# Two dense blocks on one core: the moving operand of the feature products read in lines 0, 8, 1, 9, with operands and weight parts at multiples of 1024 bytes

## What is computed

```python
h = rms_norm(x, mix_norm_pre) * (1.0 + sc1) + sh1
a_q, a_f, a_i, a_g, b_q, b_k, b_v, c_a, c_g = split_cols(h @ w_in, IN_SPLITS)
...
gates = sigmoid(h @ w_gate + b_gate)
merged = (gates[0] * (ya @ w_a_out) + gates[1] * (yb @ w_b_out) + gates[2] * (yc @ w_c_out))
x = x + g1 * rms_norm(merged @ w_o, mix_norm_post)
h = rms_norm(x, mlp_norm_pre) * (1.0 + sc2) + sh2
y = square(relu(h @ w_up)) @ w_down            # 2048 -> 8192 -> 2048
```

## Time and profile before

| | |
|---|---|
| Runs | 3234.96, 3237.93, 3238.77 us; median 3237.93 |
| Profiled execution | 3238.04 us, its span 3236.2 us |
| Granted TensorE clock | 0.996 of full speed |
| TensorE (matmul) | busy 3175.0 us, 98% of the span, 23,974 matmuls |
| VectorE | 2371.3 us, 73% |
| ScalarE | 1333.7 us, 41% |
| Weight stream | 703.64 MB, mean of all DMA 223 GB/s |

### The profile page before, as it was taken

One profiled execution on the slowest core, in us unless ns is written; L12 is line 12 of the kernel. 1 busy time (PEld: TensorE's weight loads), 2 busy tenths in 40 slices (PEclk: granted clock), 3 DMA queues, 4 the chain that ended last, 5 costly groups with the idle time before them and its releaser, 6 DMA issues.

```text
span 3236.2 us, 55394 instructions
## 1 busy us (share of the span) xinstructions
PE 3175.0 (98%) x23974; PEld 3011.5 (93%) x23974; DVE 2371.3 (73%) x2843; ACT 1333.7 (41%) x1459; POOL 1.8 (0%) x10
## 2 busy tenths in 40 slices
PE   7999999999999999999999999999999999999998
PEld 6899999999999999998988998989889989999997
DVE  5798876687887789889877766644667666767766
ACT  3333344434444433333364334421455444344444
POOL 0000000000000000000000000000000000000000
PEclk9999999999999999999999999999999999999999
DMA  9864444588794887768755763354333475655743
GB/s 396 322 215 157 158 156 150 194 324 328 301 370 153 296 310 257 267 249 287 284 191 188 285 248 144 131 218 163 118 144 131 171 260 183 224 211 197 252 167 134
DMA packets 106417, 722.62 MB, mean 223 GB/s; under 512 B 11677, under 2 KB 15389, under 8 KB 27197
## 3 DMA queue, kind: packets, MB, share of 16 engines
q1 hardware_dynamic: 100368, 703.64, 58.9%
q10 hardware_dynamic: 5806, 15.43, 1.6%
HBM read 712.41 MB, written 6.55 MB: 222 GB/s over the span
## 4 chain that ended last, share of the span: by engine, by line
PE 92%; DVE 5%; ACT 1%; DMA 1%; issue 1%; ACTq 0%; DVEq 0%
PE gemm L1040 41%; PE gemm L1049 20%; PE gemm L1076 12%; PE gemm L1079 6%; PE mix L1040 1%; DVE sb_parts L1781 1%; PE mix L1291 1%; PE mix L1571 1%; DMA sb_arena<-x_t 1%; DVE sb_arena L1836 1%; PE mix L1049 1%; PE gemm L1207 1%; PE mix L1150 1%; ACT sb_parts L539 1%; DVE sb_arena L1892 1%
## 5 line engine op out<-in xcount | busy, mean ns | idle before, releaser
L539 ACT ACTIVATE sb_parts<-sb_raw 128x2048 fp32r<-128x2048 f32 (+2 forms) x489 | 898.9, 1841 | 1533.3 <-PE gemm L1049 1005.5
L1781 DVE TENSOR_TENSOR sb_parts<-sb_raw,sb_parts 128x2048 fp32r<-128x2048 f32 (+2 forms) x489 | 1072.0, 2194 | 313.7 <-PE gemm L1049 146.0
L1040 PE MATMUL gemm<-op_h,sb_parts 128*128 128x256 f32 x7232 | 907.2, 284 | 1.0 <-ACT sb_parts L539 0.5
L1040 PEld LDWEIGHTS gemm<-op_h,sb_parts 128*128 128x128 f32 x7232 | 883.6, 192 | 2.4 <-ACT sb_parts L539 0.9
L1049 PE MATMUL gemm<-op_h,sb_parts 128*128 128x256 f32 x3616 | 470.9, 283 | 0.0
L1049 PEld LDWEIGHTS gemm<-op_h,sb_parts 128*128 128x128 f32 x3616 | 450.1, 192 | 0.1
L1076 PE MATMUL gemm<-op_up,sb_parts 128*128 128x512 f32 x1728 | 417.3, 391 | 3.0 <-DVE op_up L2410 3.0
L1076 PEld LDWEIGHTS gemm<-op_up,sb_parts 128*128 128x128 f32 x1728 | 316.5, 188 | 64.9 <-DVE op_up L2410 4.7
L1079 PEld LDWEIGHTS gemm<-op_up,sb_parts 128*128 128x128 f32 x1728 | 224.2, 191 | 9.8
L1079 PE MATMUL gemm<-op_up,sb_parts 128*128 128x256 f32 x1728 | 227.3, 283 | 0.0
L1762 DVE CUSTOM_DVE_ANT_0 sb_raw<-sb_raw,sb_arena,sb_vec 128x2048 f32<-128x2048 f32 x96 | 224.3, 2348 | 1.1
(11 more groups left out here) (360 smaller groups left out, 3427.6 us busy)
## 6 DMA issues: line engine op xcount, KB each, us to landing
sb_raw<-stream SPq DMA_DIRECT2D x597, 1024.0 KB, 5.0
sb_raw<-stream SPq DMA_DIRECT2D x64, 704.0 KB, 4.2
sb_arena<-stream SPq DMA_DIRECT2D x14, 1024.0 KB, 8.3
sb_arena<-stream SPq DMA_DIRECT2D x10, 768.0 KB, 7.8
sb_raw<-stream SPq DMA_DIRECT2D x6, 768.0 KB, 7.5
sb_arena<-c_rows ACTq DMA_DIRECT2D x3, 1024.0 KB, 7.3
bias_rows<-sb_arena ACTq DMA_DIRECT2D x1, 2304.0 KB
sb_arena<-x_t ACTq DMA_DIRECT2D x4, 512.0 KB, 18.9
```

The lines of the kernel that those rows point to most:

```text
L539: act.activation(parts[:, b % 2, 0, 0:kt, :], slot_of(slot)[:, 0:kt, :], ACT.Copy).then_inc(hi_ready, 1)
L1040: ins = pe.matmul(out, l, r, start=(opens and i == 0 and x is xh), stop=False, skip_group_check=True)
L1781: dve.tensor_tensor(parts[:, b % 2, 1, 0:kt, :], slot_of(slot)[:, 0:kt, :], parts[:, b % 2, 0, 0:kt, :].bitcast(F32), ALU.subtract).then_i ...
```

## The change

A constant `LINE` of 16 elements, 64 bytes, and a view `by_line`: it takes a row of 256 (or 512) columns as two halves of lines and orders it as line 0 of the first half, line 0 of the second, line 1 of the first, and so on. In a row of 256 columns these are the lines 0, 8, 1, 9; in one of 512 the lines 0, 16, 1, 17. The moving operand and the output of `features`, and those of both matmuls in `gemm_parts`, go through it, so each column's result lands where it did.

```diff
--- before.py
+++ after.py
@@ -16,6 +16,7 @@
 D = 2048
 KT = D // P
 SLOTS = 4
+LINE = 16
 EARLY_SLOTS, N_EARLY = 8, 48
 EPS = 1e-6
 TINY = 1e-30
@@ -370,6 +371,11 @@
         def slot_of(slot):
 
             return raw[:, slot] if slot < SLOTS else early_slots[slot - SLOTS]
+
+        def by_line(t):
+
+
+            return t.rearrange("p (b g e) -> p g b e", b=2, e=LINE)
 
         def kt_of(b):
             if b < KT:
@@ -1057,8 +1063,8 @@
 
             def features(out, op, k0=0, k1=KT, cols=slice(0, S), kw=0):
 
-                return (out, True, [(lambda w, x, k=k: (w[:, kw + k - k0, :], x), op[:, 0, k, cols], op[:, 1, k, cols])
-                                    for k in range(k0, k1)])
+                return (by_line(out), True, [(lambda w, x, k=k: (w[:, kw + k - k0, :], x), by_line(op[:, 0, k, cols]), by_line(op[:, 1, k, cols]))
+                                             for k in range(k0, k1)])
 
             def gemm_T(b, op, it=0, dn=0, cols=slice(0, S), kt=KT, waits={}):
                 product(b, [features(bank(b)[:, 0:cols.stop - cols.start], op, 0, kt, cols)], it, dn, waits=waits)
@@ -1073,10 +1079,10 @@
                     if k in waits:
                         pe.wait_ge(*waits[k])
                     both = op[:, :, k, :].rearrange("p a s -> p (a s)")
-                    pe.matmul(bank(b)[:, :], parts[:, b % 2, 0, k, :], both, start=(k == 0), stop=False, skip_group_check=True)
+                    pe.matmul(by_line(bank(b)[:, :]), parts[:, b % 2, 0, k, :], by_line(both), start=(k == 0), stop=False, skip_group_check=True)
                 pe.wait_ge(taken[slot], uses + 1)
                 for k in range(kt):
-                    ins = pe.matmul(bank(b)[:, 0:S], parts[:, b % 2, 1, k, :], op[:, 0, k, :], start=False, stop=(k == kt - 1),
+                    ins = pe.matmul(by_line(bank(b)[:, 0:S]), parts[:, b % 2, 1, k, :], by_line(op[:, 0, k, :]), start=False, stop=(k == kt - 1),
                                     skip_group_check=True)
                     if k == 0:
                         ins.then_inc(hi_used, 1)
```

## The result

| | before | after |
|---|---|---|
| Runs | 3234.96, 3237.93, 3238.77 us | 3254.8, 3257.27, 3258.97 us |
| Median | 3237.93 us | 3257.27 us |
| Profiled execution, span | 3238.04, 3236.2 us | 3258.97, 3257.2 us |

The ratio after to before is 1.0061, with a 95% interval of 1.0038 to 1.0084: slower by 0.6%, 19 us. The forecast was 3115 us, 123 us less than before; the result lies in the range and on the other side of no change.

A forecast was written before the change was run, and what follows sets the result against it. The prediction took TensorE, by its matmul count times spacing, to bound the kernel. It summed 3238.0 less 127 (8 ns off each changed matmul) plus 4 for VectorE to 3115 us, range 3080 to 3350.

The forecast's parts named there:

- TensorE bounds, and the spacing goes into the time at once: Whole kernel: time is the number of matmuls times their spacing, if VectorE, ScalarE and the weight stream keep up.
- The 4 us that the forecast gave back to VectorE: In `down1`: VectorE, nearly full, would give back 0.15 us per pair, over 24 pairs about 4 us.
- the 380 GB/s: Weight stream from 860 to 960 us: 7% faster asks for 380 for 354 GB/s, below 396, so nothing charged.
- The surcharge of 13.3 ns is partly a clash with the load of the next weights: TensorE matmuls: part of the 13.3 ns comes from weight load and moving stream meeting; 8 ns of it removable.
- by 512 bytes or a divisor of it: Reads of weights and moving operand: the clash repeats with addresses at that period; no separate size in the text.
- The position modulo 512 advances at the pace of the weights: Moving operand in the new order: it keeps pace with the weight load; no separate size in the text.
- The price of one: Each changed matmul: 8 ns less, 120 to 112 ns in 256 columns and 227 to 219 in 512.
- the dear end: End towards a loss, changed matmuls: 0.42 ns per break, 6.2 and 12.9 ns per matmul, 110 us in all.
- a saving of 127 us: All changed matmuls: 14,112 x 8 = 112.9 us plus 1,728 x 8 = 13.8 us, 126.7 us in all.
- The bound for the breaks: From token products with one break, 119.9 ns each: one break costs under a nanosecond, 0.42 ns not visible there.
- Rival 3: Changed matmuls: each break, read or written, costs a cycle and the clash stays; 3238 + 110 = 3348 us, chance 0.32.
- Rival 2: Changed matmuls: surcharge belongs to the change of weights, or clash goes by pieces under 64 bytes; 3238 us, chance 0.18.

The follow-up runs named there:

- shift64_timed: Kernel before, natural order, weight parts 64 bytes further on, timed: 3156.81 us, median of five; ratio to the kernel before 0.9761.
- line8: Changed kernel with LINE 8 in place of 16, twice the breaks: 3.3 ns more per 256-column matmul and 3.6 per 512-column one; its time is not in the text.
- quarters: Changed kernel with rows as four quarters in place of two halves, in both widths: 3217.04 us (one run), spacing 117.9 and 231.8 ns.
- line64: Changed kernel with LINE 64 in place of 16, lines of 256 bytes: nothing left of the effect in either direction; its time is not in the text.
- line32: Changed kernel with LINE 32 in place of 16, fewer breaks: takes the time of the kernel before, 14 us less in 256 columns, 13 us more in line 1082.
- write_only: Changed kernel with only the output in the new order, moving operand read in natural order: 3238.53 us (one run), beside 3241.38 us for the kernel before.

## Why the prediction was wrong, point by point

**TensorE bounds, and the spacing goes into the time at once: right.** 20.6 us of longer spacing make 20.9 us of time, and in `shift64_timed` 82 of 90 us of shorter busy time come through. The 4 us that the forecast gave back to VectorE never came due in the changed kernel, since no matmul got faster. It was an estimate: in the 11.13 us of the earlier trace rows VectorE is busy for 10.63, and no run has a `down1` stage with both widths 8 ns faster. Nor did a run ask for the 380 GB/s: from 640 to 700 us the kernel before has 503 matmuls and 324 GB/s, and `shift64_timed` 531 and 352.

**The surcharge of 13.3 ns is partly a clash with the load of the next weights: borne out as far as the runs go.** A shift of the weights alone by 64 bytes brings it from 13.3 to 7.5 ns in the mean, and half the weight columns (with half the output rows) to 7. That these are two reads in each other's way is the simplest account of it, not a thing that a run shows directly. A fixed surcharge would be the same at all six addresses; four different spacings (120.0, 118.3, 114.2 and 118.8 ns), and 2.4% of the time between two of the addresses, are against it. The forecast also took the surcharge as 13.3 ns in both widths. In 512 columns it was 15.4 in the mean (228.7 less 213.3), because the first matmuls of a group stand further apart: 232 ns for the first four, 227 for the last twelve.

**The clash goes "by 512 bytes or a divisor of it": right as worded, and too loosely used.** The spacings are the same at 0 and 256 bytes (120.0 ns) and differ at the four shifts between (114.2 to 118.8), so the divisor is 256. "The position modulo 512 advances at the pace of the weights" holds for 256 as well, so this was not what failed. But an effect that goes by address asks for a shift of the address, and that lever I didn't look at.

**"The price of one" is the step that failed.** It held that a moving operand that keeps the weights' pace adds nothing, so that both widths gain 8 ns (120 to 112, 227 to 219), and it let the breaks cost 0.42 ns each at the dear end, the time of one column (106 ns by 256 in the earlier trace rows; called a cycle there, which no row shows). Measured are 120.0 ns, nothing gained, in 256 columns, and 239.8 ns, 11.1 more than the 228.7 before, in 512. In place of a saving of 127 us stands a loss of 20.6. The term left out is what reading in this order costs by itself: 26.7 ns in 512 columns, and in 256 a spacing that stays 13.3 ns over the columns even where the shift has taken the old surcharge down. Over 32 and 16 lines that is 0.83 ns for each line, twice my bound (and no constant, as `line8` and `quarters` show). In 256 columns it ends where the old surcharge ended, at 120.0, and an exchange of one for the other would show nothing. That the two are equal is a coincidence as far as these runs tell. Whether the clash as such is gone in the new order stays open, since the order's own cost lies on top of it.

**Why the rows misled.** Line 1173 and line 1503, on which I took the 112 ns, have fp32 moving operands read in one piece. They show the spacing of a load, 111.7 and 112.5 ns, beside a slow moving stream (line 1623, also fp32, has 216 ns for 256 columns); they say nothing of a fast one read in an interleaved order. The bound for the breaks came from the earlier trace rows, a single break in 256 columns, which cannot show 0.83 ns beside other differences of that size; and its runs are 512 bytes long, where even `line64`, with a break every 256 bytes, shows nothing. The cost shows at 128 bytes (`line32`) and below.

**The rivals.** Rival 3, slower by breaks on top of a clash, was right in its sign and in that the lines cost, and wrong in the rest: I worked it out at +110 us, spread over all 15,840 matmuls, and let writing count as well as reading; it was 21 us, 19 of them in the 1,728 of line 1082, and by reading alone. Rival 2, no change, describes the other 14,112 matmuls in their spacing, but not by its reason: the surcharge does go by address. Outputs in pieces of 64 bytes, which rival 3 also charged, cost nothing: `write_only` has 120.0 and 228.7 ns, those of the kernel before.

**What stays open.** Why an interleaved read costs an eighth, whether for 256 columns that cost would also stand with fewer weight columns or at other shifts, what picks one of two spacings at the same addresses, why quarters cost less than halves and eighths, why 32 weight columns gave 117.8 ns, and why matmuls of 512 columns lose with every shift that helps those of 256. A layout with weights 64 bytes off for the feature products and not for the high parts of the down products wasn't tried.

## What to carry to other kernels

Where TensorE is full and its matmuls stand further apart than their columns (here 120.0 ns for an estimated 106.7), first try moving the weights by less than 256 bytes, with no other edit. Here a pad of 64 bytes gave 2.4%, one of 32 bytes 0.5%, and an access pattern made for the same purpose lost 0.6%. Be wary of reading the moving operand in interleaved runs under 256 bytes: here, in two halves, they cost as much as they could have saved or more (120.0 and 239.8 ns in lines of 64 bytes), and the best of them, in quarters, gained 0.3% where it was timed. Pieces of 64 bytes in the output cost nothing in `write_only` (120.0 and 228.7 ns). Time each matmul shape by itself: 240 ns beside 120, and in `line32` a loss and a gain of 13 and 14 us, stand behind times that look like little or no change. And before counting on a gain from removing a stall, ask what the new pattern costs when the stall isn't there.

## What the runs showed that I had not expected

- The address of the weights, by as little as 16 bytes, changes the spacing of 256-column matmuls whose moving operand hasn't moved: 120.0, 118.3, 118.3, 114.2, 118.8 and 120.0 ns at 0, 16, 32, 64, 128 and 256 bytes.
- The same kernel at the same addresses runs a whole stage at 117.8 ns a matmul in one execution and at 113.3 in another.
- The same shift works in opposite directions on two widths: 256 columns 120.0 to 114.2 ns, 512 columns 228.7 to 233.0 ns.
- The new order has 120.0 and 240 ns, with or without the shift by 64 bytes, and the 240 also with 64 weight columns.
- Line 1082 as before within the changed kernel is a little quicker than in the kernel before, 227.4 for 228.7 ns, though its own edit is undone. Why was not tested.
